# Segment sums of the decay as two float32r products per bank, and the high part of the LRU weights made by ScalarE

## The reference, cut to what matters

```python
# SSD, per chunk of Q = 128 tokens, H = 16 heads in G = 2 groups of E = 8
Acs  = cumsum(dt * A, axis=2)                       # decay logs, summed along the chunk
seg  = Acs[:, :, :, None] - Acs[:, :, None, :]      # sum of the decays between j and i
Lmat = exp(where(causal, seg, -inf))
CB   = einsum('bcign,bcjgn->bcijg', Cc, Bc)
y_diag = einsum('bcijg,bcijge,bcjgep->bcigep', CB, Lmat, xdt)
# RG-LRU: conv4(u @ w_in[lru_x]) -> gates -> scan -> * gelu(u @ w_in[lru_y])
```

## Time and profile before

| | |
|---|---|
| Median of 3 runs | 2294.48 us (2293.94 to 2294.68) |
| The profiled execution, its own time | 2294.69 us |
| Its span, first to last instruction | 2293.0 us |
| Instructions in it | 31925 |
| TensorE busy | 2250.4 us, 98% |
| VectorE busy | 1019.1 us, 44% |
| GpSimd busy | 754.0 us, 33% |
| ScalarE busy | 449.8 us, 20% |
| Mean granted TensorE clock | 0.997 of full speed |
| The eight slots | about 943 to 1260 us after the start |

### The profile page before, as it was taken

How to read it: one execution, slowest core, us unless ns; L and a number is a source line. 1 busy time by engine, 2 the same in 40 slices (tenths; PEclk the granted TensorE clock), 3 DMA queues, 4 the chain that set the end, 5 groups by cost and what they waited for, 6 DMA issues and landing times.

```text
span 2293.0 us, 31925 instructions
## 1 busy us (share of the span) xinstructions
PE 2250.4 (98%) x14313; PEld 2192.8 (96%) x14313; DVE 1019.1 (44%) x795; ACT 449.8 (20%) x560; POOL 754.0 (33%) x418
## 2 busy tenths in 40 slices
PE   7999999999999999999999999999999999999997
PEld 7999999999999999988888999999999999999997
DVE  5422122311233557867778586773231123212236
ACT  4100000000002225554453440120000001000102
POOL 4333333333333223343544542323333333333340
PEclk9999999999999999999999999999999999999999
DMA  4111111111112322310110422111111111111112
GB/s 141 52 50 47 47 47 47 47 47 47 47 42 79 129 75 92 113 52 31 49 42 27 172 82 86 47 46 47 47 47 47 47 46 47 47 47 47 47 55 74
DMA packets 48311, 138.86 MB, mean 61 GB/s; under 512 B 7592, under 2 KB 16296, under 8 KB 48176
## 3 DMA queue, kind: packets, MB, share of 16 engines
q1 hardware_dynamic: 47024, 135.78, 18.6%
q10 hardware_dynamic: 1152, 1.05, 0.1%
HBM read 118.19 MB, written 18.79 MB: 60 GB/s over the span
## 4 chain that ended last, share of the span: by engine, by line
PE 88%; DVE 7%; DVEq 2%; issue 1%; ACT 1%; DMA 1%; SPq 0%; ACTq 0%
PE set L556 82%; PE set L779 1%; DVEq L1288 1%; DVE lru_conv L1154 1%; PE pair L681 1%; PE set L681 1%; PE pair L689 1%; DVEq L1252 0%; DVE x L1410 0%; DVE xbc L1258 0%; DVE e L1253 0%; PE set L576 0%; DVE power L1291 0%; DVEq L1256 0%; PE set L714 0%
## 5 line engine op out<-in xcount | busy, mean ns | idle before, releaser
L452 POOL TENSOR_SCALAR w_hi<-w_raw 128x1024 fp32r<-128x1024 f32 (+1 forms) x182 | 193.6, 1064 | 1432.2 <-PE set L556 1236.4
L556 PE MATMUL set<-x_hi,w_hi 128*128 128x344 f32 x2112 | 450.2, 322 | 12.4 <-DVE x_lo L1057 12.4
L454 POOL TENSOR_TENSOR w_lo<-w_raw,w_hi 128x1024 fp32r<-128x1024 f32 (+1 forms) x182 | 445.8, 2450 | 26.8
L556 PE MATMUL set<-x_lo,w_hi 128*128 128x344 f32 x2112 | 448.9, 321 | 0.0
L556 PE MATMUL set<-x_hi,w_lo 128*128 128x344 f32 x2112 | 446.8, 320 | 0.0
L556 PEld LDWEIGHTS set<-x_hi,w_hi 128*128 128x128 f32 x2112 | 356.7, 188 | 13.1 <-issue 10.4
L556 PEld LDWEIGHTS set<-x_lo,w_hi 128*128 128x128 f32 x2112 | 358.3, 189 | 0.0
L556 PEld LDWEIGHTS set<-x_hi,w_lo 128*128 128x128 f32 x2112 | 352.8, 188 | 0.0
L1053 DVE TENSOR_TENSOR up<-set,rstd 128x1032 f32<-128x1032 f32 x43 | 53.0, 1233 | 419.7 <-PE set L556 419.7
L556 PE MATMUL set<-u_hi,w_hi 128*128 128x344 f32 x864 | 198.9, 338 | 12.4 <-DVE gelu L1053 5.5
L556 PE MATMUL set<-h_hi,w_hi 128*128 128x344 f32 x948 | 201.2, 321 | 0.8 <-DVE h_lo L1077 0.8
(11 more groups left out here) (242 smaller groups left out, 2582.9 us busy)
## 6 DMA issues: line engine op xcount, KB each, us to landing
w_raw<-in_gate_up SPq DMA_DIRECT2D x88, 512.0 KB, 3.6
w_raw<-in_w_in SPq DMA_DIRECT2D x36, 512.0 KB, 4.2
w_raw<-in_down SPq DMA_DIRECT2D x32, 512.0 KB, 3.5
w_raw<-in_w_out SPq DMA_DIRECT2D x16, 512.0 KB, 3.8
w_raw<-in_down SPq DMA_DIRECT2D x16, 384.0 KB, 3.1
x<-in_xt SPq DMA_DIRECT2D x8, 516.0 KB, 8.4
x_kept<-x SPq DMA_DIRECT2D x8, 516.0 KB, 4.9
mixed<-power SPq DMA_DIRECT2D x8, 516.0 KB, 2.9
```

Source lines behind the costliest of these rows:

```text
L452: pool.tensor_scalar(w_hi[s][:, 0:n], w_raw[s][:, 0:n], 1.0, 0.0, ALU.mult, ALU.add)
L454: pool.tensor_tensor(w_lo[s][:, 0:n], w_raw[s][:, 0:n], w_hi[s][:, 0:n].bitcast(F32), ALU.subtract).then_inc(split, 1)
L556: end = pe.matmul(out[:, c, 0:CH], w[s][:, k * P:(k + 1) * P], x[:, kx, c * CH:(c + 1) * CH], start=(first and n == 0), stop=(last and n = ...
```

## The change: what it does

The decay `a_tok` is split into `a_hi` (float32r) and `a_lo` (the rest), which take the place of `dtw`. GpSimd makes two sets of terms for each chunk: `segr` from `a_hi`, now float32r, and `segr_lo[g]` from `a_lo`, one 128x1024 instruction for each group, at the place of `lmat[g]`. `seg(g)` makes each bank's sum as two float32r products with `later_r`, a float32r copy of `later`. TensorE waits for both low sets ahead of `seg(0)`. For the units `("lx", 1)` to `("lx", 7)` ScalarE makes `w_hi` with a copy after its first tap of slot c, and GpSimd makes only `w_lo`, still after `y_done`.

```diff
+        later_r = sb("later_r", [P, P], F32R)
+        a_hi, a_lo = dtw[:, :, 0:HEADS], dtw[:, :, HEADS:2 * HEADS]
...
-        segr = at("seg_terms", Y, [HEADS, QC])
+        segr = at("seg_terms", Y, [HEADS, QC], F32R)
+        segr_lo = [at(f"seg_low{g}", Y + 2 + g, [GH, QC], F32R) for g in range(GROUPS)]
...
             def split_unit(name):
...
-                pool.wait_ge(landed[s], 16 * (u // 2 + 1))
-                pool.tensor_scalar(w_hi[s][:, 0:n], w_raw[s][:, 0:n], 1.0, 0.0, ALU.mult, ALU.add)
-                pool.drain()
+                if name[0] == "lx" and name[1]:
+                    pool.wait_ge(lx_high, name[1])
+                else:
+                    pool.wait_ge(landed[s], 16 * (u // 2 + 1))
+                    pool.tensor_scalar(w_hi[s][:, 0:n], w_raw[s][:, 0:n], 1.0, 0.0, ALU.mult, ALU.add)
+                    pool.drain()
                 pool.tensor_tensor(w_lo[s][:, 0:n], w_raw[s][:, 0:n], w_hi[s][:, 0:n].bitcast(F32),
                                    ALU.subtract).then_inc(split, 1)
...
             def seg_terms(c):
                 if c:
                     pool.wait_ge(seg_done, 2 * c)
+                    pool.wait_ge(y_done, 2 * c)
                 else:
-                    pool.wait_ge(dt_ready, 1)
+                    pool.wait_ge(a_split, 1)
+                    pool.wait_ge(xbc_ready, XT)
                 pool.tensor_tensor(segr[:], tri[:].unsqueeze(1).broadcast_to([P, HEADS, QC]),
-                                   a_tok[:, c, :].unsqueeze(2).broadcast_to([P, HEADS, QC]), ALU.mult).then_inc(segr_ready, 1)
+                                   a_hi[:, c, :].bitcast(F32).unsqueeze(2).broadcast_to([P, HEADS, QC]), ALU.mult)
+                for g in range(GROUPS):
+                    mine = a_lo[:, c, g * GH:(g + 1) * GH].bitcast(F32)
+                    pool.tensor_tensor(segr_lo[g][:], tri[:].unsqueeze(1).broadcast_to([P, GH, QC]),
+                                       mine.unsqueeze(2).broadcast_to([P, GH, QC]), ALU.mult).then_inc(segr_ready, 1)
...
-                        pe.wait_ge(segr_ready, c + 1)
+                        pe.wait_ge(segr_ready, 2 * c + 2)
                     for n in range(2):
-                        h = g * GH + 4 * n
-                        end = pe.matmul((set1 if g else pair)[:, n, :], later[:],
-                                        segr[:, h:h + 4, :].rearrange("p h t -> p (h t)"), start=True, stop=True)
+                        for low, part in enumerate((segr[:, g * GH + 4 * n:g * GH + 4 * n + 4, :],
+                                                    segr_lo[g][:, 4 * n:4 * n + 4, :])):
+                            end = pe.matmul((set1 if g else pair)[:, n, :], later_r[:],
+                                            part.rearrange("p h t -> p (h t)"), start=(low == 0), stop=(low == 1))
...
                 first_tap(XT + c, lraw, lacc)
+                if c < NCH - 1:
+                    u = U(("lx", c + 1))
+                    act.wait_ge(used, u - 1)
+                    act.wait_ge(landed[u % 2], 16 * (u // 2 + 1))
+                    act.activation(w_hi[u % 2][:], w_raw[u % 2][:], ACT.Copy).then_inc(lx_high, 1)
...
+                dve.wait_ge(consts, 1)
+                dve.tensor_copy(later_r[:], later[:])
                 dve.wait_ge(dtw_landed, 16)
...
                                          ALU.mult, ALU.mult).then_inc(dt_ready, 1)
+                dve.drain()
+                dve.tensor_copy(a_hi, a_tok[:, 0:NCH, :])
+                dve.drain()
+                dve.tensor_tensor(a_lo, a_tok[:, 0:NCH, :], a_hi.bitcast(F32), ALU.subtract).then_inc(a_split, 1)
```

More of the change, by code:

```diff
@@ L290, in build @@
             sem(n) for n in ("decode_scale", "decode_terms", "state_new", "dec_y"))
-        segr_ready = sem("seg_terms_ready")
+        segr_ready, a_split, lx_high = sem("seg_terms_ready"), sem("a_split"), sem("lru_weights_high")
         x_turned, xdt_ready, b_turned, b_read, cb_ready = (
```

## The result

| | before | changed |
|---|---|---|
| Median | 2294.58 us (4 runs) | 2311.27 us (2309.47 to 2311.74, 4 runs) |
| Ratio to before, 95% interval | | 1.0073 [1.0059, 1.0086] |
| Profiled execution, its own time | 2294.69 us | 2311.31 us |
| Its span | 2293.0 us | 2308.4 us |
| Mean granted TensorE clock | 0.997 | 0.993 |

The forecast was 2302 with a range of 2282 to 2310. The sign was right, the size was not: the change costs more than twice the 7.1 us of the sum, and the time lies above the range.

What follows compares the result with a forecast made beforehand. Each slot was taken as a serial loop, TensorE then VectorE. Ahead of slot 0 +2.7, products -10.6 and the turn +15.0 gave +7.1 us on 2294.69, so 2302, range 2282 to 2310.

Steps and rivals of the forecast that it cites:

- The products: TensorE's seg(g) sums: four passes take 0.94 us instead of 1.72, 1.56 saved per slot; 10.6 saved in slots 1 to 7.
- The close race of L1276: Slots 3 to 7: lru_power (L1276) comes 0.02 us ahead of the skip product and ends 1.5 us earlier; lost, 2306.
- GpSimd's new order in the turn: Between slots: w_lo holds the scan, segr holds the copy; 2.5 us lost in each of six slots, 15.0 together.
- the turn: VectorE's stretch from the end of L1258 to the end of L1291: 6.62 us before, 9.1 to 9.3 forecast.
- the scan was to show a record of over 4 us: In the turn, a sign: the scan, held by w_lo, would show over 4 us in the trace.
- Ahead of slot 0: Before lx(0) is scaled: GpSimd's low sets, splits and skip product hold VectorE 3.5 us, 0.8 of it slack; 2.7 lost.
- The rivals: Three other outcomes: VectorE goes first, 2282.6 us (0.15); issue order, 2315 (0.13); the two cancel, 2294 (0.10).
- VectorE never won the gap: Rival in the turn: scan or copy wins against GpSimd's waiting instruction, -0.7 us in six slots, 2282.6; chance 0.15.
- the issue-order rival: In the turn: L1286 alone follows w_lo, then segr before the scan; +4.7 us in six slots, 2315; chance 0.13.
- In the turn VectorE already ends last, so TensorE hides nothing of the 2.5: In the turn: the 2.5 us added per slot counts in full, in six slots, 15.0 us.

Runs made afterwards that it cites:

- experiment 3: The changed kernel, with GpSimd waiting for the product L1291 before it makes the terms: 2293.64 us, ratio 0.9996.
- experiment 6: The kernel before with ScalarE's high part, and one float32 set of terms made only after the product L1291: 2291.82 us, ratio 0.9988.
- experiment 8: The changed kernel with the two low sets issued ahead of the high set: 2300.19 us, ratio 1.0021.
- experiment 7: experiment 3 with the high set of chunk 0 made early, behind the split of xbc unit 6: 2290.29 us, ratio 0.9978.
- Experiment 4: The changed kernel with 12 more float32r products on TensorE ahead of the gate products of slots 1 to 6: 2300.33 us, ratio 1.0026.
- Experiment 1: The changed kernel, but GpSimd makes the high part of all weights again: 2295.03 us, ratio 1.0006.
- experiment 2: The kernel before, with only ScalarE making the high part of lx 1 to 7: 2321.6 us, ratio 1.0117.

## Why the prediction was wrong, step by step

- **The products**: right. 0.92 to 0.94 us per seg(g) as worked out (0.94), and 1.6 us per slot reached the loop. The close race of L1276 was won: the same instruction (now L1301) took 1.23 or 1.24 us in slots 3 to 7, not 2.87.
- **GpSimd's new order in the turn**: right in its order and its length. w_lo first, scan at its solo length behind it, seg_terms in the drain's gap, the copy of 3.36 us (forecast some 3.5), a turn of 9.26 (forecast 9.1 to 9.3). The term was 15.0 and measured 15.8. Experiments 3, 6 and 8 change only what stands in that gap, and the copy follows each time. One sign was wrong: the scan was to show a record of over 4 us. The 8-column L1311 takes the hold (2.40 us), and the scan, issued when w_lo is done, has a record of 2.28.
- **Ahead of slot 0**: right, 2.7 forecast and 3.1 measured, from holds of 3.5 forecast and 3.6 measured; experiment 7 shows the cause. The sum is closer than its parts: four holds grew, by 0.5, 1.5, 1.9 and 1.5 us, and one of 1.2 us that the kernel before has is gone.
- **The rivals**: none of them. VectorE never won the gap. Of the issue-order rival the first half occurred (L1286 was held by w_lo, unlike by w_hi before), but the scan followed it at once. The Trainium skill, page "SBUF — State Buffer", section "Who interferes with whom", names the exclusive port behind the holds; the whole lengths of the held instructions agree with it.
- **What failed** is the sentence "In the turn VectorE already ends last, so TensorE hides nothing of the 2.5". It prices 2.6 us more of idle TensorE at 2.6 us. The runs show that an idle time of 3.4 us ahead of lx also makes the next matmuls run at 1.2 GHz, in 16 of 18 turns of three profiles, mostly at about 1.55 us each (1.3 to 2.8), and that it does not happen after 0.2 to 1.7 us (48 turns of the eight other runs). That is 6.0 of the missing 9.6 us in the first profile and 10.2 us in the second. The forecast took the granted clock of 0.997 as given and had neither a term nor a rival for it. The Trainium skill, page "TensorE: Matmul & The Clock Gate", section "What's actually happening", says that the clock's level follows how busy the engine has lately been. Experiment 4 agrees with it: 0.58 us of idle time in place of 3.37, and no slow start. The trace of before could not show it, since its idle times ahead of lx are 0.73 to 1.09 us and no slot there starts slow.
- **The other 3.1 us** are the two stretches of half clock in the xbc units. The idle time of 2.55 us ahead of the first of them stands in both kernels (a wait for dt_rows), and only in some profiles does half clock follow: in the changed kernel's first profile and in experiments 3 and 6, not in its second one, nor in the kernel before. So no run shows that the change causes them. In the second profile of the changed kernel they are absent and two more slots start slow instead, at the same median; why the sum comes out alike stays open.
- **Experiment 1** corrects a thought behind the sum. I expected the products' saving and the turn to be independent. They are not: GpSimd's instructions hold VectorE somewhere in each slot, and the changed kernel kept its 1.6 us per slot because it had put seg_terms into the turn.

## What to carry to other kernels

When two engines exclude each other, count the time of an engine's queue, not only its busy share: freeing 1.09 us of GpSimd in each of six turns cost 27 us in experiment 2. The instructions behind it moved up by one place: w_lo came in front of the scan and a 3.6 us one in front of a 9-column copy on the chain (15.8 us), and the longer idle time of TensorE brought the half clock (10.4 us). Place long instructions of the other engine by a wait, where the chain's engine has idle time or reads PSUM: in experiment 3 the scaling of ly, which reads PSUM, took its usual 1.23 us beside seg_terms (3.61 us). And price added idle time of TensorE at more than its length: here 3.4 us of it were followed by half clock in 16 of 18 turns, 0.2 to 1.7 us in none of 48.

## What the runs showed that was not expected

- Twelve useless products of 512 columns ahead of the gates, in six slots, made the changed kernel 10 to 11 us faster (2310.26 or 2311.27 to 2300.33).
- A held series counts one instruction at a time: of 3.6 + 1.9 + 1.9 us of terms waiting at the scan's end, the copy waited only for the first (3.36 or 1.64 us).
- The same 2.55 us of idle time ahead of an xbc unit was followed by 27 matmuls of 4.51 to 4.54 us in nine profiles and of 6.05 to 6.07 us in three, with the same instructions around it.
